# Gate projection directly behind layer 0's memory keys, with layer 0's memory values and key square sums moved behind the step sizes

## What is computed

```python
def mem_kv(mem, norm_g, wk, wv, k_norm_g):            # mem: 256 tokens x 1024, once per layer
    hm = rmsnorm(mem, norm_g)
    mk = rmsnorm((hm @ wk).reshape(bsz, m, 4, 128), k_norm_g)
    mv = (hm @ wv).reshape(bsz, m, 4, 128)
    return mk, mv

def mixer_even(h, ...):                               # h = rmsnorm(x, norm_mix_g[0])
    a_val, a_gate, z, xbc, dt_raw = split(h @ w_in)   # 512, 512, 512, 1024, 8 columns
    a_conv = causal_dwconv(a_val * sigmoid(a_gate))   # 31 taps, 512 channels
    a_out = silu(layernorm(a_conv))
    xs, b_in, c_out = split(silu(causal_dwconv(xbc))) # 4 taps, 1024 channels
    dt = softplus(dt_raw + dt_bias)
    y = ssd_scan(xs, dt, -exp(a_log), b_in, c_out)    # the scan
    return concat([a_out, grouped_rmsnorm((y + d_skip * xs) * silu(z))]) @ w_out
```

## Time and profile before

| | us |
|---|---|
| median of the three timed runs | 1725.58 |
| the three runs | 1724.09, 1725.60, 1725.58 |
| the profiled execution, whole | 1724.31 |
| its span from the first to the last instruction | 1722.3 |
| mean granted TensorE clock of the span | 0.995 |

### The profile page before, as it was taken

The page is one execution under the profiler, slowest core; times in us unless marked ns, Lnnn a source line. Parts: engine busy times, 40 slices in busy tenths (PEclk is TensorE's granted clock), DMA queues, the critical chain, the costliest instruction groups (busy, mean ns, idle before and its releaser), DMA issues.

```text
span 1722.3 us, 28510 instructions
## 1 busy us (share of the span) xinstructions
PE 1679.3 (98%) x11696; PEld 1591.6 (92%) x11696; DVE 1061.5 (62%) x1709; ACT 717.8 (42%) x1288; POOL 417.7 (24%) x327
## 2 busy tenths in 40 slices
PE   7999888999999999999999999999999999999999
PEld 6989876897999999999989898789799999999999
DVE  3899877547677646465654335654666774655564
ACT  4322564244434435253542135533543452534352
POOL 3424511221004233232223033100110241414240
PEclk9999989999999999999999999999999999999999
DMA  8323440242213131303133223504220313122312
GB/s 265 105 90 90 124 159 7 73 192 103 86 40 127 47 130 32 129 26 129 37 130 74 75 74 110 203 27 156 113 105 19 123 48 133 44 74 84 105 49 92
DMA packets 40253, 164.96 MB, mean 96 GB/s; under 512 B 9448, under 2 KB 10344, under 8 KB 26176
## 3 DMA queue, kind: packets, MB, share of 16 engines
q1 hardware_dynamic: 32816, 127.21, 22.3%
q0 software_dynamic: 7312, 35.98, 5.7%
HBM read 152.49 MB, written 10.42 MB: 95 GB/s over the span
## 4 chain that ended last, share of the span: by engine, by line
PE 79%; DVE 5%; ACT 2%; issue 1%; DVEq 0%; ACTq 0%
PE G L991 56%; PE S L991 12%; PE Q L991 11%; PE Q L1717 1%; ACT work L1813 0%; DVE ev_low L2731 0%; ACT front L1813 0%; DVE stats L2761 0%; DVE resid L3013 0%; ACT h_split L1813 0%; PE Q L1429 0%; DVE S L2656 0%; DVE stats L3132 0%; DVE work L2774 0%; DVE w_split L2986 0%
## 5 line engine op out<-in xcount | busy, mean ns | idle before, releaser
L991 PE MATMUL G<-ffn_rows,w_split 128*128 128x320 f32 x2160 | 329.8, 309 | 0.0
L991 PEld LDWEIGHTS G<-ffn_rows,w_split 128*128 128x128 f32 x2160 | 320.1, 188 | 0.0
L1813 ACT ACTIVATE w_split<-ring 128x512 fp32r<-128x512 f32 (+2 forms) x224 | 159.1, 711 | 316.5 <-PE G L991 208.1
L907 POOL TENSOR_TENSOR mkT<-ring 128x512 f32<-128x512 f32 x72 | 98.6, 1375 | 564.5 <-DMA ring<-in_w_up 383.9
L991 PE MATMUL G<-h_split,w_split 128*128 128x320 f32 x1344 | 200.9, 310 | 1.2 <-DVE w_split L2491 0.9
L991 PEld LDWEIGHTS G<-h_split,w_split 128*128 128x128 f32 x1344 | 197.5, 188 | 1.9 <-issue 1.3
L991 PE MATMUL G<-g_split,w_split 128*128 128x320 f32 x1056 | 163.7, 310 | 0.1
L991 PEld LDWEIGHTS G<-g_split,w_split 128*128 128x128 f32 x1056 | 156.6, 188 | 1.6 <-DVE w_split L2986 1.4
L2853 DVE TENSOR_TENSOR w_split<-ring,w_split 128x512 fp32r<-128x512 f32 (+1 forms) x124 | 104.6, 845 | 60.6 <-ACT w_split L1813 59.4
L2986 DVE TENSOR_TENSOR w_split<-ring,w_split 128x512 fp32r<-128x512 f32 (+1 forms) x80 | 66.0, 825 | 115.9 <-ACT w_split L1813 115.1
L2575 DVE SCALAR_TENSOR_TENSOR S<-front,par,S 128x512 f32<-128x512 f32 x232 | 107.0, 543 | 0.1
(11 more groups left out here) (365 smaller groups left out, 3269.5 us busy)
## 6 DMA issues: line engine op xcount, KB each, us to landing
ring<-in_w_up SPq DMA_DIRECT2D x44, 1024.0 KB, 4.8
ring<-in_w_down SPq DMA_DIRECT2D x48, 256.0 KB, 2.6
ring<-in_w_down SPq DMA_DIRECT2D x32, 320.0 KB, 2.9
front<-in_mem_k POOLq DMA_DIRECT2D x8, 1024.0 KB, 6.9
front<-in_mem_v POOLq DMA_DIRECT2D x8, 1024.0 KB, 11.2
resid<-in_x SPq DMA_DIRECT2D x8, 640.0 KB, 9.3
ring<-in_w_mk SPq DMA_DIRECT2D x4, 1024.0 KB, 5.9
ring<-in_w_mv SPq DMA_DIRECT2D x4, 1024.0 KB, 10.9
```

What stands on the lines that cost most here:

```text
L907: nc.gpsimd.tensor_tensor(wsum[n], a, b, ALU.subtract).then_inc(sum_ready, 1)
L991: return nc.tensor.matmul(out, lhsT, rhs, start=start, stop=stop, **kw)
L1813: return nc.scalar.activation(*a, **k)
```

## The change

The gate tiles stand directly behind layer 0's key tiles; between the two there is only the square sum of x. Layer 0's memory values with all four key sums move between narrow_sum and layer 1's values. The tables of tiles, chunks, squares and norms follow that order. The sum of the memory's squares moves from behind key tile 1 to behind key tile 0. On ACT the squares of x start behind memory_scales, with key tile 1 read in their middle and key tiles 2 and 3 behind them; the squares and inverse roots of layer 0's keys stand behind those of layer 1's. On DVE the sums of x's squares come first, then layer 1's memory rows, and the four add_key_eps stand among the convolution's taps behind step_sizes: 10 taps, eps 0, 6 taps, eps 1, 10 taps, eps 2, 6 taps, eps 3. On POOL layer 0's key norms follow layer 1's. Further down conv_stat(3) moves from behind front tile 14 to behind 12, and ACT's order of xbc reads, first taps, activations, z gates and weight parts is changed to fit. No instruction is added or dropped.

```diff
-for _n, _c in (("mk0", 4), ("mv0", 2), ("glu", 8), ("dtp", 1), ("mk1", 4), ("dt", 1), ("mv1", 2), ("xbc", 8),
+for _n, _c in (("mk0", 4), ("glu", 8), ("dtp", 1), ("mk1", 4), ("dt", 1), ("mv0", 2), ("mv1", 2), ("xbc", 8),
-for _n, _c in (("mem", 8), ("mk0", 4), ("x", 8), ("mk1", 4), ("mean", 0), ("var", 4), ("gn", 0), ("evout", 8), ("q0", 4), ("wo0", 8),
+for _n, _c in (("mem", 8), ("x", 8), ("mk1", 4), ("mk0", 4), ("mean", 0), ("var", 4), ("gn", 0), ("evout", 8), ("q0", 4), ("wo0", 8),
-_memory("0")
+_chunks("mk0", 2, WCH, _pairs("mk0"))
 _chunks("glu", 4, WCH, _pairs("glu"))
-_memory("1")
+_chunks("mk1", 2, WCH, _pairs("mk1"))
+_memory_values("0")
+_memory_values("1")
-                for i in range(l * MH, (l + 1) * MH):
-                    key = mkT[:, l, i % MH, :]
-                    pool.wait_ge(rstd_ready, i + (3 if l else 2))
-                    nc.gpsimd.tensor_tensor(key, key, rstd[:, (i + (0 if l else 1)) % 2, 0:MT], ALU.mult).then_inc(pool_self, 1)
+                for j in range(MH):
+                    i = (1 - l) * MH + j
+                    key = mkT[:, l, j, :]
+                    pool.wait_ge(rstd_ready, i + 3)
+                    nc.gpsimd.tensor_tensor(key, key, rstd[:, i % 2, 0:MT], ALU.mult).then_inc(pool_self, 1)
...
-            memory_keys(0)
             for n in range(1, 3):
                 front_low(n)
...
             memory_keys(1)
+            memory_keys(0)
             for n in range(8, 10):
                 front_low(n)
-                    if l == 0 and n == 1:
+                    if l == 0 and n == 0:
-                    if n >= 2 - l:
-                        key_stat(l, n - 2 + l)
+                    if l and n >= 1:
+                        key_stat(l, n - 1)
-                beside = [{}, {}] if l else [{2: lambda: key_stat(0, 2), 5: lambda: key_stat(0, 3)},
-                                             {5: lambda: residual_stat("x")}]
+                beside = [{}, {}] if l else [{2: lambda: key_stat(0, 0), 5: lambda: key_stat(0, 1)},
+                                             {2: lambda: key_stat(0, 2), 5: lambda: key_stat(0, 3)}]
             memory_keys(0)
-            memory_values(0)
+            residual_stat("x")
             front_plain()
             for n in range(1, 8):
                 front_project(n)
             narrow(TILE0["dtp"], "wdt", x_hi[:, :, :].bitcast(F32), h_lo[:, :, :].bitcast(F32))
             memory_keys(1)
             narrow_sum(TILE0["dt"], TILE0["dtp"], dt_parts)
+            memory_values(0)
             memory_values(1)
             for n in range(8, 18):
                 front_project(n)
-                if n == 14:
+                if n == 12:
                     conv_stat(3)
-            for j in range(4):
-                n, key = TILE0["mk0"] + j, mkT[:, 0, j, :]
-                evacuate(key, n, width=MT)
-                if j == 1:
-                    memory_scales()
-                read_wait(act, n)
-                square(key, MT)
-                if j == 2:
-                    inv_std(1, 1.0 / P, 5, MT)
-            for j in range(1, 4):
-                inv_std(1, 1.0 / P, 5, MT)
+            def first_key(j):
+                evacuate(mkT[:, 0, j, :], TILE0["mk0"] + j, width=MT)
+
+            first_key(0)
+            memory_scales()
             for k in range(KD):
                 act.wait_ge(x_in[k // 2], 16)
                 square(x[:, k, :])
+                if k == 3:
+                    first_key(1)
+            first_key(2)
+            first_key(3)
...
-            memory_values(0, 0)
+            residual_inv_std(2)
             act.wait_ge(applied, APPLIED["mem"])
             front_high_part(1)
-            residual_inv_std(2)
-            memory_values(0, 1)
             head_norms(lambda j: mkT[:, 1, j, :], TILE0["mk1"], 4, 1.0 / P, MT)
+            for j in range(2):
+                read_wait(act, TILE0["mk0"] + j)
+                square(mkT[:, 0, j, :], MT)
+            for j in range(2, 4):
+                inv_std(1, 1.0 / P, 5, MT)
+                square(mkT[:, 0, j, :], MT)
+            memory_values(0, 0)
+            for j in range(2):
+                inv_std(1, 1.0 / P, 5, MT)
+            memory_values(0, 1)
...
+            xbc_first(0)
+            xbc_first(1)
             xbc_rows(4)
             front_high_part(14)
-            xbc_first(0)
-            xbc_first(1)
+            conv_mean()
             xbc_rows(5)
             front_high_part(15)
-            xbc_rows(6)
-            front_high_part(16)
-            conv_mean()
-            xbc_rows(7)
-            front_high_part(17)
             log_exp_table()
             act.wait_ge(cs_ready, 1)
             A(dtb[:, 2, :], dtb[:, 2, :], ACT.Exp, scale=-1.0).then_inc(de_ready, 1)
             nc.scalar.preload_act_table_set("silu_and_others")
+            xbc_rows(6)
+            front_high_part(16)
             xbc_silu(0)
-            z_gate(0)
-            front_high_part(18)
             xbc_silu(1)
             act.wait_ge(applied, APPLIED["mean"])
             for k in range(4):
                 square(acc[:, k, :])
+            xbc_rows(7)
+            front_high_part(17)
             xbc_silu(2)
+            z_gate(0)
+            front_high_part(18)
+            xbc_silu(3)
+            xbc_silu(4)
             z_gate(1)
             front_high_part(19)
             log_exp_table()
@@ -2070,11 +2082,10 @@
             A(toks[:, :, :, :].rearrange("p a b c -> p (a b c)"), G[n % 2][:, 0:2 * NCH * NH], ACT.Copy)
             A(decay[:, :, :].rearrange("p a b -> p (a b)"), G[n % 2][:, 512:512 + NSEG * NH], ACT.Exp)\
                 .then_inc(read[n % 2], 1)
-            for j in range(3, 5):
+            for j in range(5, 7):
                 xbc_silu(j)
             z_gate(2)
-            for j in range(5, KD):
-                xbc_silu(j)
+            xbc_silu(7)
             z_gate(3)
+            nnorm[0] += 1
+            for j in range(KD):
+                add_square("x", j)
-            add_key_eps(0)
-            add_key_eps(1)
-            add_key_eps(2)
-            add_key_eps(3)
-            nnorm[0] += 5
             step_sizes()
+            for j in range(4):
+                conv_taps(6 if j % 2 else 10)
+                add_key_eps(j)
             conv_taps(8 * CW - taps_done[0])
```

More of the change, by code:

```diff
@@ L91 @@
 APPLIED, NORM, _a, _m = {}, [], 0, 0
-for _n, _c in ([("mem", 8)] + [(f"mk0.{j}", 0) for j in range(4)] + [("mix0", 8)] + [(f"mk1.{j}", 0) for j in range(4)]
+for _n, _c in ([("mem", 8), ("mix0", 8)] + [(f"mk{l}.{j}", 0) for l in (1, 0) for j in range(4)]
                + [("mean", 4), ("var", 4), ("gn0", 2), ("gn1", 2), ("cross0", 8)]
@@ L178, in _cross_ffn, with _memory_values @@
         _chunks(down, KD, n * P, _pieces(down, 1))
-def _memory(l):
-    _chunks("mk" + l, 2, WCH, _pairs("mk" + l))
+def _memory_values(l):
     _chunks("mv" + l, 2, WCH, lambda i: ("tile", TILE0["mv" + l] + 2))
-_memory("0")
+_chunks("mk0", 2, WCH, _pairs("mk0"))
 _chunks("glu", 4, WCH, _pairs("glu"))
-_memory("1")
+_chunks("mk1", 2, WCH, _pairs("mk1"))
+_memory_values("0")
+_memory_values("1")
 _chunks("xbc", 4, WCH, _pairs("xbc"))
@@ L2523, in _ @@
                                        in1=rstd[:, 0, 0:MT], op0=ALU.mult, op1=ALU.mult).then_inc(applied, 1)
-            add_key_eps(2)
-            add_key_eps(3)
-            nnorm[0] += 5
             for i in range(KD // 2):
                 dve.wait_ge(x_in[i], 16)
-            for j in range(KD):
-                add_square("x", j)
             norm_x("mix0")
@@ L2538, in _ @@
                 v.tensor_tensor(h_lo[:, k, :], h[:, k, :], x_hi[:, k, :].bitcast(F32), ALU.subtract).then_inc(mix_low, 1)
-            nnorm[0] += 4
+            nnorm[0] += 8
             def step_sizes():
```

## The result

The changed kernel takes 1727.32 us (median of 20 runs, 1726.17 to 1728.52), the kernel before 1724.86 us (20 runs, 1722.34 to 1726.65): a ratio of 1.0016 with a 95% interval of 1.0009 to 1.0023. It is 2.5 us slower, less than the 0.2% that I called no change; 1728.2 us was forecast. The two profiled executions lie further apart, 1728.52 (span 1726.6) against 1724.31 (span 1722.3), 4.3 us. That matters where rows of the two are subtracted.

A forecast was written before the change was run, and what follows sets the result against it. PE, busy 98%, was taken as the bound. Late waits -4.31 and -2.1, z_gate -2.3, new waits with clock +9.2, gate clock +2.1 gave +2.6 on 1725.6: 1728.2 us, range 1721 to 1734.

The forecast's parts named there:

- case (a): The forecast itself, with or without gate clock and port: -2 to +3.4 us, 1723.5 to 1729; chance 0.6.
- Part 1: Front of layer 0: sum of x and gate start 16.1 us earlier, with a PE wait of about 2.8 us.
- Part 2: Layer 0's values in their new place: PE waits 7.6 us for eps 0, plus low clock behind it.
- rival (c): Faster: the wait for eps 0 is off the path; -8.5 us, half version about -3; chance 0.12.
- The gate's clock: First gate tile: low clock behind PE's 2.8 us wait costs 0 or 2.1 us; 2.1 taken.
- The port: Risk at DVE's first square sum beside POOL: POOL's part 1.6 us later, and PE waits as long.
- Part 3: xbc and z tiles: late waits go, PE ends the stage; z_gate(3) +0.5 us, +2.6 us with the gate's clock.
- small moves: Chunk loads, POOL key norms, conv_stat and ACT order: covered or same instructions; 1 to 2 us wait if uncovered.
- The scan's clock: At the scan the clock may stay up, saving up to 1.6 us; taken as 0.
- Rival (b): Slower: low clock in the values lasts until the third eps; +5.5 us, 1731, with the port 1733; chance 0.28.

The follow-up runs named there:

- e1: Changed kernel with each add_key_eps ahead of its convolution taps instead of behind them; 1722.04 us, ratio 0.9986.
- e4: Changed kernel with 20 taps instead of 10 before eps 0; 1732.43 us, ratio 1.0044.
- e2: Changed kernel with layer 0's four key sums one value tile later on PE, ACT's order to match; 1719.17 us, ratio 0.9969.
- e3: Changed kernel with three added, unread matmuls on PE between the sum of x and the first gate tile; 1726.72 us, ratio 1.0014.
- e8: Changed kernel with key sums one value tile later, ACT's old order from the xbc tiles on and conv_stat(3) back behind tile 14; 1726.6 us, ratio 1.0017.
- c0: The changed kernel run again with no edit, beside the kernel before; 1727.63 us, ratio 1.0023.
- e5: Changed kernel with ACT's old order from the xbc tiles on and conv_stat(3) back behind tile 14; 1734.5 us, ratio 1.0054.
- e6: Kernel before with only the change's new ACT order from xbc_rows(0) to z_gate(3) and conv_stat(3) moved to 12; 1727.06 us, ratio 1.001.
- e7: Changed kernel with key sums one value tile later and three unread matmuls before the gate; 1717.55 us, ratio 0.9956.
- e9: Changed kernel with later key sums, and the sum of x ahead of steps 6 and 7 of key tile 3; 1718.55 us, ratio 0.9968.
- e11: Kernel before with a milder ACT reorder: activations and z gate 0 earlier, the mean's sum still at 14; 1725.02 us, ratio 1.0.

## Why the prediction was right

The number held: 2.5 us slower was measured, 2.6 forecast, in case (a). (In absolute terms the forecast is 0.9 us high, since the median of three runs it started from, 1725.58, was 1724.86 over twenty.) The new wait and its place were right, and it makes most of the sum. But one gain had the wrong cause and three terms were off in size, and these errors cancelled, so that a hit within 0.1 us is in part luck.

- **Part 1** held. Sum of x 26.60 (forecast 26.35), first gate step 31.68 (31.45), wait 2.76 (2.8), the wait of 1.36 us moved along; DVE's first gating is at 49.40 (49.6 with low clock).
- **Part 2** held. Key sum 0 is reached at 117.4 instead of 115.2, 1.7 us of it from the slower gate tile, which the sum had as a term of its own; eps 0 ends at 124.24, 1.4 us later than drawn. The wait is 6.91 instead of 7.6 us, and of the other three no more than tenths are seen. e1, e4 and e2 show that it is paid in full: rival (c), the wait off the path, is excluded. Its price with the clock is the difference of the changed kernel and e2, 8.2 to 8.5 us (1727.32 and 1727.63 less 1719.17); the sum had 9.2.
- **The gate's clock** was a term of 2.1 us; it is mis-sized. The tile took 10.54 us, 1.7 more than before, and of those 1.1 are there at full clock too (e3). The clock's part was 0.6 us here. The same 2.76 us wait cost no clock in e2, e4 and e8 and did in the changed kernel, c0, e1 and e5 (there the tile took 11.87 us). The Trainium skill, TensorE: Matmul & The Clock Gate, section HAM oscillation, has work behind a wait of PE restart at half rate, in its example behind longer waits than this one. The prediction read it as holding for the 2.8 us too, which the page does not say. The window at 34 (0.50) came out that way all the same; in e2, behind the same 2.76 us, the stretch did not:

```profile
33.00:35.00 2.00, 1.88 (x8) 0.90 (x6) 2.00 (x2) 0.74 (x1) 2.00 (x2) 1.00 0.88 196
35.00:37.00 2.00, 1.53 (x7) 0.94 (x6) 2.00 (x3) 1.22 (x2) 0.01 (x1) 1.00 0.82 207
```

- **The port** was looked for at the square sum, where it did not come (0.83 us at 211.81, against 2.39 in the earlier trace rows). It came at the norm rows, where I had not looked. DVE's and POOL's timelines of the changed kernel:

```profile
30.65 8.49 DVE L2454 SCALAR_TENSOR_TENSOR front<-resid,par,rstd 128x640 f32<-128x640 f32 x8 [1.78 <-ACT rstd L1816]
```

```profile
31.64 3.63 POOL L823 TENSOR_TENSOR ring_split<-ring,front_r 128x512 fp32r<-128x512 f32 x2 [5.04 <-ACT front_r L1816]
```

The eight rows took 6.46 us before, with POOL's part done by then (43.99 to 46.49, so 2.50 us); beside it they take 8.49, and POOL's part 3.63 us. The Trainium skill, SBUF — State Buffer, section SBUF: two separate sides, says that a DVE operation with two SBUF inputs and a GpSimd operation that reads SBUF exclude each other. Both rows growing at once agrees; no run took POOL's part away to show it alone.

- **Part 3 had the wrong cause.** The prediction read POOL's wait as "itself behind the convolution on DVE"; in the kernel before ACT's first activation of xbc stood behind the read of xbc tile 7, so behind PE (201.06 and 206.23 above). It took the late waits as falling "only if nothing else is late" by DVE's 16 us, and under small moves I wrote that "conv_stat and the ACT order have the same instructions", so at no cost or gain. e5 and e8 show that without ACT's new order both waits stay at 4.3 and 3.3 us, and that the old order costs 7 us; e6 shows that the order without the head start pays 7.59 us elsewhere. The two parts are worth something only together (1719.2 us in e2). It used the new order for its times (xbc_silu(0) at about 206; it came at 206.41) but gave it no share of the gain. The step as written would have put e5 where the changed kernel is, 7 us too fast.
- **The scan's clock** was taken as 0, with -1.6 for the range. In the profiled pair it went the other way: 18.51 us instead of 15.96. Over the eleven profiles in which PE arrives with a wait of 1.0 us (c0, e1 to e4, e6, e7, e9 to e11 and the first), the stretch took 15.69 to 18.51 us, in the middle one 17.55; in the three with the old order, which arrive with 3.34 or 3.35 us, 15.65 to 15.96. This term is about +1.6 us in the middle, with a spread of 2.8 us.
- **Compensation.** In the profiled pair the stage ended 1.77 us later, not 2.6, and the scan took 2.55 us more, not 0. Against c0's profile it is +3.45 and -0.2. The gate's and the eps wait's terms were too large and the scan's too small by about as much.
- **Rival (b)** had the low clock last through DVE's pacing in the values. In the first profile it was 0.50 from 122 to 128 and 0.84 at 128 to 130, so low for some 4.4 us behind the wait's end, and no longer; at half rate that is 2.2 us, as forecast. Its condition, low clock until the third eps (132), was not met. It came nearer in c0: 0.50 until 131, 6 us behind the wait's end, and the twelve matmuls there took 5.28 us instead of 4.41. Whether the three runs of c0 at 1731 us are this rival stays open.

## What to carry to other kernels

A reorder that frees one engine must be judged by the first cross-engine operand that the bound engine now meets: here a 0.4 us instruction, placed behind ten taps, ate the gain of 8 us, and moving its readers one tile later gave a kernel 0.3% faster than the one before. On in-order queues, test the parts of a change as a two-by-two table before giving one of them the credit: a head start on one engine was idle time here (20.8 us on DVE) until the order of the others let it through. When a wait disappears ahead of a stage with gaps of its own, look where the clock will fall next.

## What was not expected of the hardware

- Arriving at full clock can be worse than arriving at low clock: after a wait of 3.34 us in front of the scan, its first part took 15.7 to 16.0 us; after 1.0 us, with the 3.1 us gap still to come, 15.7 to 18.5 us. That the low clock moves onto denser matmuls is read from the windows of two profiles; it was not isolated by a run.
- Equal waits are not equal: behind the same 2.76 us wait the granted clock fell in four profiled executions and stayed up in three, and the first gate tile took 9.98 to 11.87 us. What decides it stays open.
